# Gate tiles among the first convolution tiles, with their low parts made by GpSimd

## The reference, cut to what matters

```python
hn = rmsnorm(h, norm1_w[l])
proj = hn @ w_in[l]
gates, z, xbc, dt_raw, lru_x, lru_y = jnp.split(proj, IN_SPLITS, axis=-1)
gates = jax.nn.sigmoid(gates + b_branch_gate[l])
g_ssm, g_lru = jnp.split(gates, 2, axis=-1)
y_ssm = mamba2_mixer(z, xbc, dt_raw, ...) @ w_out_ssm[l]
y_lru = rglru_mixer(lru_x, lru_y, ...) @ w_out_lru[l]
h = h + (g_ssm * y_ssm + g_lru * y_lru) @ w_out[l]
```

## Time and profile before

| | |
|---|---|
| median of 3 runs | 1224.34 us |
| profiled execution | 1222.55 us, of which span 1221.2 us |
| busy: PE, DVE, ACT, POOL | 97%, 66%, 57%, 23% of the span |
| mean granted clock of TensorE | 0.993 |
| PE matmul instructions | 7688 |

### The profile page before, as it was taken

How to read it: one execution, slowest core, us unless ns; L and a number is a source line. 1 busy time by engine, 2 the same in 40 slices (tenths; PEclk the granted TensorE clock), 3 DMA queues, 4 the chain that set the end, 5 groups by cost and what they waited for, 6 DMA issues and landing times.

```text
span 1221.2 us, 18874 instructions
## 1 busy us (share of the span) xinstructions
PE 1185.9 (97%) x7688; PEld 1057.7 (87%) x7688; DVE 810.9 (66%) x1044; ACT 697.3 (57%) x962; POOL 278.9 (23%) x181
## 2 busy tenths in 40 slices
PE   9798999999999999999999899999999989999997
PEld 9798999999998888888999688888899977888886
DVE  7878988677566866676878455555456973555454
ACT  6788766675535443435646856445554397555543
POOL 0000000001401111111475522122225654222211
PEclk9899999999999999999999999999999999999999
DMA  9444756544546665554643346665464533575560
GB/s 294 162 123 155 240 175 197 184 138 163 203 161 235 207 202 176 200 176 139 196 133 122 104 140 208 204 193 183 161 189 140 170 105 108 176 230 184 182 207 34
DMA packets 152437, 210.66 MB, mean 172 GB/s; under 512 B 5504, under 2 KB 132640, under 8 KB 151712
## 3 DMA queue, kind: packets, MB, share of 16 engines
q1 hardware_dynamic: 151584, 205.08, 51.8%
q10 hardware_dynamic: 768, 4.39, 1.0%
HBM read 208.37 MB, written 1.08 MB: 172 GB/s over the span
## 4 chain that ended last, share of the span: by engine, by line
PE 78%; ACT 10%; DVE 8%; issue 2%; DMA 1%; POOL 0%; SPq 0%; ACTq 0%; DVEq 0%
PE banks L534 76%; ACT w_hi L1008 3%; ACT tmp L1008 2%; DVE w_lo L1398 2%; ACT L1008 2%; PE banks L542 1%; DVE xbc L1406 1%; ACT probs_dil L1008 1%; DMA raw<-in_w_in 1%; DVE work L1402 1%; ACT lru_ab L1008 1%; ACT probs_dsa L1008 0%; DVE tmp L1406 0%; ACT xbc L1008 0%; DVE lru_u L1406 0%
## 5 line engine op out<-in xcount | busy, mean ns | idle before, releaser
L534 PE MATMUL banks<-act,w_hi 128*128 128x256 f32 (+1 forms) x3216 | 731.9, 317 | 14.0 <-DVE w_lo L1398 11.6
L534 PEld LDWEIGHTS banks<-act,w_hi 128*128 128x128 f32 x3216 | 524.1, 191 | 62.9 <-issue 18.2
L534 PE MATMUL banks<-act,w_lo 128*128 128x256 f32 (+1 forms) x2040 | 562.2, 282 | 0.0
L1398 DVE TENSOR_TENSOR w_lo<-raw,w_hi 128x2048 fp32r<-128x2048 f32 (+4 forms) x174 | 377.0, 2168 | 215.1 <-ACT w_hi L1008 214.5
L1008 ACT ACTIVATE w_hi<-raw 128x2048 fp32r<-128x2048 f32 (+1 forms) x191 | 359.6, 1884 | 187.2 <-PE banks L534 184.3
L534 PEld LDWEIGHTS banks<-act,w_lo 128*128 128x128 f32 (+1 forms) x2040 | 382.7, 191 | 1.4
L534 PE MATMUL banks<-w_hi,act 128*128 128x512 f32 (+1 forms) x1072 | 322.9, 376 | 7.0 <-DVE act L1398 6.5
L1996 POOL TENSOR_TENSOR act<-tmp,act 128x512 fp32r<-128x512 f32 x52 | 112.6, 2169 | 706.5 <-ACT act L1008 706.5
L534 PEld LDWEIGHTS banks<-w_hi,act 128*128 128x128 f32 x1072 | 197.2, 190 | 46.7 <-issue 11.0
L1996 POOL TENSOR_TENSOR w_lo<-raw,w_hi 128x512 fp32r<-128x512 f32 (+1 forms) x120 | 156.1, 1330 | 204.1 <-ACT w_hi L1008 204.1
L534 PE MATMUL banks<-w_lo,act 128*128 128x512 f32 (+1 forms) x536 | 200.0, 373 | 0.0
(11 more groups left out here) (228 smaller groups left out, 732.8 us busy)
## 6 DMA issues: line engine op xcount, KB each, us to landing
raw<-in_w_in SPq DMA_DIRECT2D x64, 1024.0 KB, 5.3
raw<-in_w_up SPq DMA_DIRECT2D x32, 1024.0 KB, 5.4
raw<-in_w_down SPq DMA_DIRECT2D x32, 1024.0 KB, 5.1
raw<-in_w_ffn_in SPq DMA_DIRECT2D x22, 1024.0 KB, 5.1
raw<-in_w_out SPq DMA_DIRECT2D x12, 1024.0 KB, 5.0
raw<-in_w_ffn_out SPq DMA_DIRECT2D x11, 1024.0 KB, 5.0
raw<-in_w_out_ssm SPq DMA_DIRECT2D x8, 1024.0 KB, 5.1
raw<-in_w_out_lru SPq DMA_DIRECT2D x5, 1024.0 KB, 4.9
```

The source lines that it names most:

```text
L534: return mm_ops.matmul(out, lhs, rhs, start=start, stop=stop, skip_group_check=True)
L1398: return ops.tensor_tensor(out, a, b, op)
```

## The change

The order of the tiles up to z changes. Three of the eight gate tiles move among the lx and bc tiles, and ly and xs tiles change places:

| position | 3 | 4 | 5 | 6 | 7 | 8 | 9 | 10 | 11 | 12 | 13 | 14 | 15 | 16 | 17 | 18 |
|---|---|---|---|---|---|---|---|---|---|---|---|---|---|---|---|---|
| before | lx2 | lx3 | lx4 | bc0 | bc1 | bc2 | bc3 | xs0 | xs1 | xs2 | ly0 | gate0 | xs3 | ly1 | gate1 | xs4 |
| after | lx2 | gate0 | lx3 | lx4 | gate1 | bc0 | bc1 | gate2 | bc2 | bc3 | xs0 | xs1 | xs2 | ly0 | xs3 | gate3 |

After position 30 both orders are the same. The stages move with the tiles: `gates_ready` from lx2 (3) to gate0 (4), `dt_cs` from bc1 (7) to bc2 (11), `dt_turn` from bc3 (9) to bc3 (12), the first `ssd_open` from position 15 to 16, and the last `ssd_val` from z4 to z5. GpSimd makes the whole low part of every gate tile, and all gate tiles go through `columns_low_last`. The gates get memory of their own (shared with the part of `act` that the first three tiles read), and y, the input of the state-space output product, goes to a new tensor `late` that shares its place with the finished recurrence.

```diff
@@ tile_names
-    names += [("lx", j) for j in range(5)]
-    names += [("bc", j) for j in range(4)]
-    names += [("xs", 0), ("xs", 1)]
-    for j in range(5):
-        names += [("xs", 2 + j), ("ly", j), ("gate", j)]
-    names += [("xs", 7)] + [("gate", j) for j in range(5, 8)]
+    names += [("lx", 0), ("lx", 1), ("lx", 2), ("gate", 0), ("lx", 3), ("lx", 4), ("gate", 1), ("bc", 0), ("bc", 1),
+              ("gate", 2), ("bc", 2), ("bc", 3), ("xs", 0), ("xs", 1), ("xs", 2)]
+    for j in range(4):
+        names += [("ly", j), ("xs", 3 + j), ("gate", 3 + j)]
+    names += [("xs", 7), ("ly", 4), ("gate", 7)]
@@
-POOL_SHARE = {
+POOL_SHARE = {"gate": 8,
@@ stage_order
-    put("mid", ("lx", 2), ("gates_ready",))
-    for tile, heads in ((("lx", 3), (0, 1)), (("lx", 4), (2, 3))):
+    put("mid", ("gate", 0), ("gates_ready",))
+    for tile, heads in ((("lx", 3), (0, 1)), (("lx", 4), (2, 3)), (("gate", 1), (4, 5, 6)), (("bc", 0), (7,)),
+                        (("bc", 1), (8,)), (("gate", 2), (9,))):
         put("mid", tile, *[("lru", h) for h in heads])
...
-    places = TILES[T["xs", 3]:T["z", 4] + 1]
+    places = TILES[T["ly", 0]:T["z", 5] + 1]
@@ pe_program
-                        (columns_low_last if i < LOW_LAST else columns)(i, name, j, base, ring)
+                        (columns_low_last if i < LOW_LAST or name == "gate" else columns)(i, name, j, base, ring)
@@ act_program
                 if name == "gate":
-                    act.wait_ge(*at("lru_scan", 2 * (j % 5) + 2))
                     act.wait_ge(*at("halved", 3))
```

More of the change, by code:

```diff
@@ L191, in put @@
         order.setdefault((where, T[tile]), []).extend(stages)
-    put("mid", ("lx", 2), ("gates_ready",))
-    for tile, heads in ((("lx", 3), (0, 1)), (("lx", 4), (2, 3))):
+    put("mid", ("gate", 0), ("gates_ready",))
+    for tile, heads in ((("lx", 3), (0, 1)), (("lx", 4), (2, 3)), (("gate", 1), (4, 5, 6)), (("bc", 0), (7,)),
+                        (("bc", 1), (8,)), (("gate", 2), (9,))):
         put("mid", tile, *[("lru", h) for h in heads])
-    put("mid", ("bc", 0), ("lru", 4), ("lru", 5))
-    put("mid", ("bc", 1), ("dt_cs",), ("lru", 6), ("lru", 7))
-    put("mid", ("bc", 2), ("lru", 8))
-    put("mid", ("bc", 3), ("dt_turn",), ("lru", 9))
-    put("mid", ("xs", 0), ("lru_root", 0))
-    put("mid", ("xs", 1), ("lru_root", 1))
+    put("mid", ("bc", 2), ("dt_cs",))
+    put("mid", ("bc", 3), ("dt_turn",), ("lru_root", 0))
+    put("mid", ("xs", 0), ("lru_root", 1))
     for j in range(5):
-        put("mid", ("xs", 2 + j), ("lru_scan", 2 * j), ("lru_scan", 2 * j + 1))
+        put("mid", ("gate", 2 + j) if j else ("xs", 2), ("lru_scan", 2 * j), ("lru_scan", 2 * j + 1))
     ssd = []
@@ L341, in build @@
         res = sb("residual", [P, TT, D])
+        with ExitStack() as shared:
+            sb("act_first", [P, 8, 2, SEQ], F32R, stack=shared)
+            gates = sb("gates", [P, 2 * DC, SEQ], stack=shared)
         both_parts = sb("act", [P, 16, 2, SEQ], F32R)
@@ L364, in build @@
         lru_u = sb("lru_u", [P, LC, SEQ], stack=one)
-        lru_ab = sb("lru_ab", [P, 2 * LC, SEQ], stack=one)
-        lru_a, lru_b, gates = lru_ab[:, 0:LC, :], lru_ab[:, LC:2 * LC, :], lru_ab[:, 0:2 * DC, :]
+        with ExitStack() as shared:
+            lru_ab = sb("lru_ab", [P, 2 * LC, SEQ], stack=shared)
+        late = sb("late", [P, 2 * LC, SEQ], F32R, stack=one)
+        lru_a, lru_b = lru_ab[:, 0:LC, :], lru_ab[:, LC:2 * LC, :]
+        y_hi, y_lo, last_hi, last_lo = late[:, 0:8, :], late[:, 8:16, :], late[:, 16:18, :], late[:, 18:20, :]
         cs_all = sb("cs_all", [P, HPG, SEQ], stack=one)
@@ L722, in rows_ready @@
                     pe.wait_ge(*at("y_lo", j + 1))
-                    return 8 + GC * (j // 2 % 2) + 2 * (j % 2)
+                    return GC * (j // 2 % 2) + 2 * (j % 2)
                 if name == "out_lru":
@@ L754, in rows @@
                     return token_rows(i, name, j, whole, first, last, ring, hi, lo, k0)
+                x_hi, x_lo = (y_hi, y_lo) if name == "out_ssm" else (act_hi, act_lo)
+                if (name, j) == ("out_lru", 4):
+                    x_hi, x_lo, k0 = last_hi, last_lo, 0
                 for b in range(DC // 2):
@@ L762, in rows @@
                             inst = product(bank[:, m * SEQ:(m + 1) * SEQ], hi[:, j2, c0:c0 + P], lo[:, j2, c0:c0 + P],
-                                           act_hi[:, k0 + j2, :], act_lo[:, k0 + j2, :], first and j2 == 0 and m == 0,
+                                           x_hi[:, k0 + j2, :], x_lo[:, k0 + j2, :], first and j2 == 0 and m == 0,
                                            last and j2 == 1)
@@ L1182, in norm_split @@
                 for s in range(2):
-                    k = 8 + GC * (g % 2) + 2 * s
+                    k = GC * (g % 2) + 2 * s
+                    act.wait_ge(*at("lru_scan", LC))
                     act.wait_ge(*at("gn_x", 2 * g + s + 1))
@@ L1996, in tt, with low_part @@
                 return nc.gpsimd.tensor_tensor(out, a, b, op)
-            def low_part(k, n, src):
-                return tt(act_lo[:, k:k + n, :], src, act_hi[:, k:k + n, :].bitcast(F32), ALU.subtract)
+            def low_part(k, n, src, hi=act_hi, lo=act_lo):
+                return tt(lo[:, k:k + n, :], src, hi[:, k:k + n, :].bitcast(F32), ALU.subtract)
             split = {"next": 0}
@@ L2027, in norm_split @@
                     pool.wait_ge(*at("y_hi", 2 * g + s + 1))
-                    low_part(8 + GC * (g % 2) + 2 * s, 2, pair(tmp[8 + s][:, :])).then_inc(*tick("y_lo"))
+                    low_part(GC * (g % 2) + 2 * s, 2, pair(tmp[8 + s][:, :]), y_hi, y_lo).then_inc(*tick("y_lo"))
             def lru_split(n):
                 pool.wait_ge(*at("lru_hi", n + 1))
-                low_part(2 * n, 2, lru_u[:, 2 * n:2 * n + 2, :]).then_inc(*tick("lru_lo"))
+                src = lru_u[:, 2 * n:2 * n + 2, :]
+                (low_part(0, 2, src, last_hi, last_lo) if n == 4 else low_part(2 * n, 2, src)).then_inc(*tick("lru_lo"))
             pool.wait_ge(*at("x1_hi", 3))
```

6 lines of the change are left out of this document (3 added, 3 removed).

## The result

The changed kernel took 1227.89 us (median of 6 runs, 1227.37 to 1229.78), beside 1223.95 us for the kernel before in the same comparison: a ratio of 1.0037, 95% interval 1.0027 to 1.0047. It is slower by 4.5 us (3.3 to 5.8) by the ratio, 3.9 us by the medians; the forecast was 1222.7 us, 1217.5 to 1227.5. The profiled execution took 1227.49 us with a span of 1226.2 us.

A forecast was written before the change was run, and what follows sets the result against it. TensorE was 97% busy, losing time from 26 to 122 us, where a loop between ScalarE and VectorE sets the pace. 5.4 + 0.1 - 0.7 - 2.1 - 1.1 = 1.6 us won gave 1222.7 us, range 1217.5 to 1227.5.

The forecast's parts named there:

- Where the time would be: TensorE's one stretch to win in was 26 to 122 us, where 19.1 us were lost; 160 to 330 us had 0.7.
- The wait of 5.87 us: TensorE's wait before bc0, near 50 us, the largest piece lost; it was to go, with a clock of 1.00 there.
- head 6: In gate1, TensorE was to wait 3.3 us for lx3's convolution, whose opening stands behind heads 0 and 1 on ScalarE.
- signs of being wrong: Tile 15 at 110 us or less, TensorE waiting for GpSimd's low parts, or new waits behind 165 us.
- Term one: Up to the end of position 16, without GpSimd's holds: TensorE at 130.1 us instead of 135.5, 5.4 us won.
- The walk: Trace times moved into the new order from ScalarE's high part of tile 5, at 38.63 us, first without GpSimd's disturbance.
- I take the middle: GpSimd holding VectorE, midpoints of ranges: gate0 0.1 us sooner, gate2 0.7 later, gate3 1.1 later; gate1 nothing.
- every hold lands: Second rival listed: all GpSimd holds cost time, at gate0's start and beside gate3's scans; 1226.5 us, chance 0.20.
- Term two: First masks: `cs` load lands at 136.1 us, second `ssd_val` 2.5 us late; 2.7 - 0.6 = 2.1 us lost.
- Nothing lost behind 160 us: Remaining edits hit no wait from 160 to 330 us: nothing, or some 0.5 us if later masks push group norms.
- The clock: Rival: new waits halve TensorE's clock, 2.8 us each; unswallowed at `ssd_open` or in the masks, 1225.5 us; chance 0.07.
- The rival of the quicker loop: Waits for head 6, `cs` and `ssd_open` halve, 5 us more won, about 1216 us; chance 0.10.

The follow-up runs named there:

- a1: The changed kernel, but VectorE makes the low parts of all gate tiles; 1222.76 us, ratio 0.9993 to before.
- d2: Old tile order with VectorE's gate low parts and the new buffers; only ScalarE's spill of `cs` moves, from bc1 to bc3; 1218.70 us, ratio 0.9965 to before.
- c3: Old tile order, VectorE's gate low parts, new buffers; `cs` summed behind `gates_ready`, spilled in bc0, loaded in xs1; 1219.57 us, ratio 0.9971 to before.
- d1: The changed kernel, but ScalarE's spill of `cs` moves from bc2 to xs0, VectorE's sum staying in bc2; 1222.98 us, ratio 1.0009 to before.
- b2: The changed kernel, but VectorE makes the low parts of gate0 to gate2, GpSimd those of gate3 to gate7; 1225.71 us, ratio 1.0021 to before.
- b3: The changed kernel, but GpSimd makes the low parts of gate0 to gate2 only; 1224.86 us, ratio 1.0013 to before.
- c1: The changed kernel, but only the load of `cs` is issued earlier, in xs0 instead of ly0; 1227.33 us, ratio 1.0038 to before.
- b1: The changed kernel with VectorE's gate low parts, and `cs` summed behind `gates_ready`, spilled in bc0, loaded in xs0; 1218.20 us, ratio 0.9962 to before.
- d4: b1 with both recurrence roots in xs0 and the scans of heads 2 to 9 one tile later; 1215.61 us, ratio 0.9939 to before.
- b4: b1, but head 6 of the recurrence moves from gate1 to bc0; 1219.26 us, ratio 0.9967 to before.

## Why the prediction was wrong

**Where the time would be: right but for 1.3 us.** At `ssd_val` 0,3 (168.76 us) the changed kernel is 3.6 us behind, at the second group norm 4.9. The wait of 5.87 us went, and the waits for head 6 (1.7, forecast 3.3), `cs` (3.8, forecast 3.9), `ssd_open` (0.8, forecast 2.1) and the first two masks came where they were expected. Tile 15 starts at 119.2 us, outside the 113 to 118 that were to show the forecast right, and one of its signs of being wrong came: waits behind 165 us. What TensorE doesn't use lies less in the first tenth of the span than was said ahead of the prediction: 14.9 us of 35.3 up to 122 us.

**Term one, 5.4 us without holds: about right.** The walk had `ssd_open` at 125.8 us; with all holds gone it started at 126.37 (a1), 4.8 us ahead of before. It had ScalarE's wait for the spill in it, but as a given. That this one wait cost 3 to 4 us in either order, and that a stage moved by two tiles takes it away (d2, c3, d1), I didn't see, though the earlier trace rows are of the same queue, three microseconds further on.

**The step that failed: "I take the middle" of GpSimd's holds.** Against a kernel whose gate low parts VectorE makes (5.4 - 2.1 = 3.3 us won by the prediction), the step put GpSimd's part at 3.3 - 1.6 = 1.7 us lost. It took 0.1 us won at gate0, 0.7 lost at gate2 and 1.1 at gate3, because "about half of its instructions there are taps or read PSUM". Measured: 5.4 us by the ratios (a1 against the change), and 6.4 at the second group norm of the two traces. At gate0 the taps came 1.34 us later than before and 1.5 later than with VectorE's own low part (a1); 2.4 us were lost by `ssd_open`. In the masks 5.9 us were lost with GpSimd and 2.0 without (a1), 1.5 of the difference the clock's. By b2 and b3, 2.0 us go with the early gates and 2.9 with the late ones. The reason for the half failed where it was needed: two of the three scalings next in line at gate0 and the masks at gate4 were held, and they are neither taps nor readers of PSUM. A bound that comes from a list of instructions should be settled by reading that list; the order of VectorE's queue was there to be read.

The rival "every hold lands" (1226.5, chance 0.20) came nearest, 1.4 us too low, but partly by luck. With all holds its terms give 2.0 + 1.4 + 2.1 = 5.5 us, close to the 5.4 in all, but 3.4 of them before `ssd_open`, where 2.4 were lost, and 2.1 in the masks, where it was 3.9. It had gate4's holds "counted in" and no clock in them.

**Term two, the late load of `cs`: wrong cause, right size.** 2.1 us were forecast and 2.0 lost in the masks without GpSimd (a1). But c1 issues the load 21 us sooner and wins nothing that shows, and b1 with the early load waits as long before `ssd_val` 0,1 as a1 with the late one. What made that mask late was the other thing in the same sentence, two scans ahead of it on VectorE: d4 moves them and the loss is gone.

**Nothing lost behind 160 us: wrong by 1.3 us.** Waits of 0.25 and 0.89 us in later masks, in every kernel of the new order with the scans in the gate tiles, go with 1.2 to 1.3 us between `ssd_val` 0,3 and the second group norm. The prediction costed the last stages at nothing because the stretch of before had no waits there; that says nothing of a stretch whose queue order is changed. With d4's scans 0.3 us are left.

In the traces these steps make up the whole error. 1.6 us were to be won and 4.9 were lost, 6.5 in all: 0.6 in term one, 4.7 in the holds (6.4 for 1.7), 1.3 in the later masks, and 0.1 back in term two.

**The clock: chance too low.** The forecast gave 0.07 to a fall in the masks that nothing swallows, at 2.8 us. It came, for 1.5 us, behind a wait of 3.30 us that the holds had made. The clock was no rival apart from the holds. Two earlier falls, near 42 and 104 us, were swallowed, much as the forecast had it: head 6 waits 1.7 us in the changed kernel, and 2.9 in a1, which has no fall near 42.

**Sums.** The chance of "slower", half of the second rival and half of the clock, is 0.10 + 0.035 = 0.14 and not 0.17. The rival of the quicker loop is 5 us below the forecast, so 1217.7 on the median; 1216 is what comes out from the profiled execution's 1221.0. Neither touches the forecast.

## What to carry to other kernels

Before work is given to GpSimd, list what stands next in VectorE's queue while it runs: each of its 128x512 instructions cost the one beside it up to about 1.1 us, and for 2.28 us spared at gate0 VectorE paid 3.8. A DMA that waits for another engine's result doesn't belong in the queue of an engine that sets the pace: one stage moved two tiles back won as much (4.3 us) in the old order as the reordering of fifteen tiles did with the early sum (b1, 4.6). And a wait of TensorE can be a mere symptom: one of 2.9 us was worth nothing that shows when it was moved away (b4), and 3.4 us came back while one of 3.8 us stayed (d1), since another engine's queue ended last. Last, compare traces at places of equal work, not by their spans: two waits far behind the change made single executions differ by up to 3 us.
